# Placing turned query tiles with four transfers instead of six, and turning them one unit earlier, in both attentions of a two-layer trunk

## The chip, the cores and the metric

One Trainium2 chip, one core. The metric is device time in microseconds (us) of one execution; smaller is better. The kernel before was timed three times: 3293.59, 3291.07 and 3286.45 us, median 3291.07.

## The reference, cut to what matters

The program is one step of a two-layer trunk on 1024 latent tokens and 128 context tokens. The change touches only the attention of each layer. Cut to that, the reference computes:

```python
def blocked_gqa(q, k, v):                      # layer 0: 8 query heads, 2 key/value heads, head width 64
    def one_block(qblk):                       # 128 queries at a time
        s = jnp.einsum('bqkgd,bskd->bkgqs', qblk, k) * D ** -0.5
        pr = jax.nn.softmax(s, axis=-1)
        return jnp.einsum('bkgqs,bskd->bqkgd', pr, v)

def blocked_diff_attention(q, k, v, lam):      # layer 1: 8 heads, two maps each, value width 128
    def one_block(qblk):
        s = jnp.einsum('bqphd,bsphd->bphqs', qblk, k) * D ** -0.5
        pr = jax.nn.softmax(s, axis=-1)
        w = pr[:, 0] - lam * pr[:, 1]
        return jnp.einsum('bhqs,bshe->bqhe', w, v)
```

Latent queries see 256 cached keys and 1024 latent keys (1280); context queries see the 128 context keys. Everything is float32.

## The kernel before, in words

**Split products.** A float32 factor is kept as two parts, high and low. For the scores (L1311 to L1331) the keys of a head lie in `ks` as 128 rows: 64 rows of high parts and below them 64 rows of low parts. The queries lie in `qst` for two slots `v`, and two matmuls, one per slot, add up in one PSUM tile. Before the change slot 0 holds high over low and slot 1 low over high, so that the two matmuls together form all four products of a high or low query part with a high or low key part.

**Groups, tiles, units.** `attention` (L906) is built twice. Layer 0 (`l == 0`) has two groups of four query heads that share one key head; layer 1 has four groups of two heads with two maps each. Inside a group the tokens are projected tile by tile (nine tiles of 128 tokens: eight latent, one context); then the scores, the softmax and the products with the values go by units. A unit is one head of one query tile: four units per tile in layer 0, two units of two maps in layer 1. `program` (L1037) is the order of a group and is replayed by each engine with its own functions; `unit_0` (L990) and `unit_1` (L1012) are the order inside a unit. In unit `u` TensorE (PE) makes the scores of unit `u + 1`, turns (transposes against an identity) the probabilities of unit `u - 2` (layer 0) or `u - 1` (layer 1), and makes the product with the values; in layer 0 that product and the exponentials are made in even units only, for two units at once. ACT copies the turned probabilities out of PSUM (`attn_pt`, L1429) and makes the exponentials (L1496), DVE takes the maxima (L1703), scales the probabilities (L1715) or mixes the two maps (L1721), and reads out the product (L1729, L1731). Turned things share two PSUM banks in alternation (`next_bank`, L1240): whoever takes a bank waits until what lay in it two uses ago was read.

**The way of a query tile.** `stage` on PE (L1304) transposes the queries of tile `qt` (L1308); `stage` on ACT (L1478) copies them to `q_turned` (L1483); `split_queries` on POOL (L1168) makes the high and the low part in `q_parts` (L1172, L1174), after the transfers of the tile before have landed; `place_queries` on SP (L1110) sends the parts to `qst[qt % 2]`; the first scores of the tile wait for these transfers (L1316). There are six transfers: two of 128 KB (L1117, L1118) and four of 64 KB (L1120, L1121, one per slot). Tiles 0 and 1 are staged while tokens are still projected (`STAGED_AT`). `stage_after` (L1065) says after which unit the later ones are: in layer 0 tile `t + 1` in unit `4t + 1`, in layer 1 tile `t + 2` in unit `2t + 1`.

**The queue of SP.** `group` on SP (L1123 to L1156) goes in order: loads of cached keys and values; placements of tiles 0 and 1; a wait until the weights of this group are used (L1139); the weight loads of the next group (`pre.load`, 1.5 MB in layer 0 and 3 MB in layer 1) or, in the last group, three pieces of the output weights (`out_ahead`); the stores of the new keys and values; placements of tiles 2 to 8.

```python
    def stage_after(u):
        qt = u // per_tile + (1, 2)[l]
        return qt if u % per_tile == 1 and qt >= 2 and qt < NT else None
```

## Time and profile before

| what | value |
|---|---|
| median of 3 runs | 3291.07 us (3286.45 to 3293.59) |
| the profiled execution | 3292.2 us |
| its span | 3290.4 us |
| mean granted TensorE clock | 0.984 |
| the two groups of attention 0 | about 262 to 600 us of the span |
| the four groups of attention 1 | about 1630 to 2360 us of the span |

The span runs from the first to the last instruction; the execution's own time is 1.8 us longer. Of an engine the profile gives busy time and, in the view of waits, for whom it stood idle. "PEld" is TensorE's weight load, which runs beside its matmuls ("PE"), whose ends are modelled; a wait in front of a matmul therefore shows twice, once in each, with slightly different lengths.

### The profile page before, as it was taken

How to read it: one execution, taken by the hardware profiler on the slowest of the kernel's cores; microseconds unless marked ns; L12 is line 12 of the kernel's file. 1: busy time of each engine (PE TensorE's matmuls, PEld its weight loads, DVE VectorE, ACT ScalarE, POOL GpSimd, SP SyncE). 2: the span in 40 equal slices, each digit the busy share in tenths (PEclk: the TensorE clock that was granted, in tenths of full speed). 3: DMA queues.
4: the chain of work that ended last, by engine and by line, in shares of the span. 5: the costliest groups of instructions: out<-in, count | busy, mean ns of one | idle time of the engine just before them, and what ended most of it. 6: DMA issues, size and time to landing. Idle time of an engine off the chain costs nothing. (4 is left out here: it accounts for less than half of the span.)

```text
span 3290.4 us, 55637 instructions
## 1 busy us (share of the span) xinstructions
PE 3086.6 (94%) x19944; PEld 2384.8 (72%) x19944; DVE 2218.8 (67%) x2691; ACT 1847.0 (56%) x2625; POOL 696.1 (21%) x587
## 2 busy tenths in 40 slices
PE   5998989998999999997999999999997999999999
PEld 4767777774767777675887888888885677767776
DVE  4777676557666666665777776867747766666666
ACT  3555747434666665563466483755733666566564
POOL 1101010001233223321322122222200222332221
PEclk9999999998999999999999999999998999999999
DMA  7231111439888888887021210302245888888885
GB/s 235 87 131 47 33 39 33 146 139 380 297 285 305 289 303 285 293 296 237 15 75 27 67 35 13 87 14 55 72 166 213 300 294 300 287 287 309 292 295 155
DMA packets 240092, 593.71 MB, mean 180 GB/s; under 512 B 38883, under 2 KB 90280, under 8 KB 239656
## 3 DMA queue, kind: packets, MB, share of 16 engines
q1 hardware_dynamic: 229534, 557.54, 48.2%
q0 software_dynamic: 9472, 33.57, 4.3%
q8 instruction: 109, 1.79, 0.2%
q14 instruction: 71, 0.58, 0.1%
q10 hardware_dynamic: 906, 0.23, 0.0%
HBM read 524.00 MB, written 38.94 MB: 171 GB/s over the span
## 5 line engine op out<-in xcount | busy, mean ns | idle before, releaser
L2193 DVE TENSOR_TENSOR moe_lo<-moe_raw,moeg_hi 128x2048 fp32r<-128x2048 f32 x384 | 882.2, 2325 | 289.5 <-ACT moeg_hi L2190 153.8
L2190 ACT CAST moeg_hi<-moe_raw 128x2048 fp32r<-128x2048 f32 x384 | 729.6, 1913 | 437.5 <-PE psum L2596 320.8
L1208 PE MATMUL psum<-attn_w_hi,attn_hs 128*128 128x512 f32 (+2 forms) x1424 | 370.2, 343 | 16.3 <-DVE attn_hs L1587 11.3
L1703 DVE TENSOR_REDUCE attn_neg_max<-psum 128x1 f32<-128x1280 f32 (+1 forms) x216 | 292.1, 1354 | 117.0 <-PE psum L1328 115.6
L1328 PE MATMUL psum<-attn_ks,attn_qst 128*128 128x512 f32 (+2 forms) x1200 | 305.5, 376 | 48.8 <-DMA attn_qst<-attn_q_parts 25.3
L1496 ACT ACTIVATE attn_e<-psum,attn_neg_max 128x1280 f32<-128x1280 f32 (+1 forms) x216 | 265.1, 1228 | 94.8 <-DVE attn_neg_max L1703 91.3
L1208 PEld LDWEIGHTS psum<-attn_w_hi,attn_hs 128*128 128x128 f32 x1424 | 250.8, 190 | 48.4 <-DVE attn_hs L1587 12.2
L1328 PEld LDWEIGHTS psum<-attn_ks,attn_qst 128*128 128x128 f32 x1200 | 203.1, 190 | 87.6 <-DMA attn_qst<-attn_q_parts 26.2
L2596 PE MATMUL psum<-moe_lo,moeh_x_hi 128*128 128x512 f32 x960 | 262.0, 395 | 0.0
L2596 PE MATMUL psum<-moeg_hi,moeh_x_hi 128*128 128x512 f32 x960 | 261.5, 394 | 0.0
L2596 PE MATMUL psum<-moeg_hi,moeh_x_lo 128*128 128x512 f32 x960 | 260.5, 393 | 0.0
L1208 PE MATMUL psum<-attn_w_lo,attn_hs 128*128 128x256 f32 (+2 forms) x712 | 241.4, 339 | 0.0
L2181 PE MATMUL psum<-moe_raw,moeh_xc 128*32 128x512 f32 x2048 | 234.3, 598 | 0.0
L1429 ACT COPY attn_pt<-psum 128x512 f32<-128x512 f32 (+2 forms) x400 | 190.8, 506 | 64.0 <-PE psum L1341 57.6
L2596 PEld LDWEIGHTS psum<-moeg_hi,moeh_x_hi 128*128 128x128 f32 x960 | 177.7, 188 | 51.2 <-issue 14.0
L2596 PEld LDWEIGHTS psum<-moeg_hi,moeh_x_lo 128*128 128x128 f32 x960 | 180.1, 188 | 42.3
L2596 PEld LDWEIGHTS psum<-moe_lo,moeh_x_hi 128*128 128x128 f32 x960 | 180.4, 188 | 41.1
L1341 PE MATMUL psum<-ident,attn_e 128*128 128x128 f32 x1296 | 196.3, 279 | 12.0 <-ACT attn_pt L1429 7.7
L1341 PEld LDWEIGHTS psum<-ident,attn_e 128*128 128x128 f32 x1296 | 145.5, 141 | 41.2 <-issue 20.7
L2174 POOL COPY moeh_xc<-moe_x_ctx 128x64 f32 (+1 forms) x64 | 126.5, 2007 | 217.6 <-PE psum L2181 191.5
L2486 POOL CAST moeh_x_hi<-moeh_x_tmp 128x1024 fp32r<-128x1024 f32 x30 | 32.0, 1065 | 639.9 <-ACT moeh_x_tmp L2681 639.9
L1188 POOL TENSOR_TENSOR rstd<-ssq,neg_half 128x8 f32<-128x8 f32 (+1 forms) x54 | 80.1, 1484 | 406.2 <-DVE ssq L1619 406.2
(359 smaller groups left out, 5433.1 us busy)
## 6 DMA issues: line engine op xcount, KB each, us to landing
moe_raw<-in_l_w_gate SPq DMA_DIRECT2D x256, 512.0 KB, 4.1
moe_raw<-in_l_w_up SPq DMA_DIRECT2D x256, 512.0 KB, 5.2
moe_raw<-in_l_w_down SPq DMA_DIRECT2D x128, 1024.0 KB, 6.2
ada_w<-in_l_ada_w SPq DMA_DIRECT2D x19, 1024.0 KB, 13.7
attn_qst<-attn_q_parts SPq DMA_DIRECT2D x108, 128.0 KB, 2.4
attn_qst<-attn_q_parts SPq DMA_DIRECT2D x216, 64.0 KB, 2.1
ada1h_w<-in_l_ada_w SPq DMA_DIRECT2D x9, 1024.0 KB, 10.9
lru_ada<-in_l_ada_w SPq DMA_DIRECT2D x8, 1024.0 KB, 7.7
```

The source lines that it names most:

```text
L1188: pool.tensor_tensor(m.rstd[:, 0:nz], m.ssq[:, 0:nz], m.neg_half[:, 0:nz], ALU.pow).then_inc(s["rstd"], 1)
L1208: last = pe.matmul(out, hs[t % 2][:, part, k, :], right, start=(i == 0 and n == 0), stop=(i == KB - 1 and n == 2))
L1328: last = pe.matmul(m.psum[:, into:into + step], query_map(u // per_tile, qm, v), ks[:, km, col:col + step], start=(v == 0), stop=(v == 1))
L1341: last = pe.transpose(m.psum[:, at + (i - b) * P:at + (i - b + 1) * P], src[:, i * P:(i + 1) * P], m.ident[:, :])
L1429: act.copy(out, src).then_inc(s["turn_read"], 1)
L1496: act.activation(out[:, 0:hi - lo], m.psum[:, score_at(n):score_at(n) + hi - lo], ACT.Exp, bias=neg_max[:, n:n + 1], accum_out=sums[:, n:n ...
L1703: dve.tensor_reduce(neg_max[:, n:n + 1], m.psum[:, score_at(n):score_at(n) + hi - lo], AX.X, ALU.max, negate=True).then_inc(s["maxed"], 1)
L2174: last = pool.tensor_copy(dst[:, :, j, :], mm.x_ctx[:, :, ds(e * 8 + j * P, 8)])
L2181: last = pe.matmul(m.psum[32 * g:32 * g + 32, 6 * BANK:7 * BANK], mm.xc[:, k, :], mm.raw[k][:, g // 2, (g % 2) * BANK:(g % 2 + 1) * BANK], ...
L2190: act.copy(mm.hi[slot % 4][:, :, :], mm.raw[slot][:, :, :]).then_inc(mm.s["hi_ready"], 1)
L2193: dve.tensor_tensor(mm.lo[slot][:, :, :], mm.raw[slot][:, :, :], mm.hi[slot % 4][:, :, :].bitcast(F32), ALU.subtract).then_inc(mm.s["lo_re ...
L2596: last = pe.matmul(m.psum[:, at:at + BANK], x[:, k, :], w[:, j, half * BANK:(half + 1) * BANK], start=(k == 0 and i == 0), stop=(k == KB - ...
```

## The change

It does four things in both attentions. The slots of `qst` now hold the high part twice (in both halves of the rows) and the low part twice, so a tile is placed by four transfers of 128 KB, and the counter per tile goes from 96 to 64. A tile is turned one unit sooner: in layer 0 tile `t + 1` in unit `4t`, in layer 1 tile `t + 2` in unit `2t`. Before placing tiles from 2 on, SP waits until all scores that read the buffer (those of tile `qt - 2`) are made. And on SP the stores and the placement of tile 2 come ahead of the weight loads of the next group.

```diff
@@ -980 +980 @@
-    PLACED = 6 * 16
+    PLACED = 4 * 16
@@ -1065 +1065 @@
-        return qt if u % per_tile == 1 and qt >= 2 and qt < NT else None
+        return qt if u % per_tile == 0 and qt >= 2 and qt < NT else None
@@ -1112 +1112 @@ place_queries
                 wait_value(m, sp, s["q_split"], j * NT + (qt + 1))
                 if qt == 1:
                     wait_value(m, sp, s["ssq"], j * NT + NT)
+                if qt >= 2:
+                    wait_value(m, sp, s["scored"], j * nmaps + (qt - 1) * per_tile * maps)
                 top, low = slice(0, HD), slice(HD, P)
                 to, parts = qst[qt % 2][:, :, :, :, :].bitcast(F32), q_parts[:, :, :, :].bitcast(F32)
-                sp.dma_start(to[top, 0, :, :, :], parts[top, :, :, :]).then_inc(s["q_placed"], 16)
-                sp.dma_start(to[low, 1, :, :, :], parts[low, :, :, :]).then_inc(s["q_placed"], 16)
-                for v in range(2):
-                    sp.dma_start(to[low, 0, v, :, :], parts[top, 1 - v, :, :]).then_inc(s["q_placed"], 16)
-                    sp.dma_start(to[top, 1, v, :, :], parts[low, 1 - v, :, :]).then_inc(s["q_placed"], 16)
+                for i, of in enumerate((top, low)):
+                    for half in (top, low):
+                        sp.dma_start(to[half, i, :, :, :], parts[of, :, :, :]).then_inc(s["q_placed"], 16)
@@ -1136 +1136 @@ group on SP
                 for qt in range(2):
                     place_queries(j, qt)
-                wait_value(m, sp, s["w_used"], j + 1)
-                if last:
-                    out_ahead(sp)
-                else:
-                    pre.load(sp, j + 1)
-
                 wait_value(m, sp, s["k_new"], j + 1)
                 wait_value(m, sp, s["v_copied"], j * NT + NT)
...
-                for qt in range(2, NT):
+                place_queries(j, 2)
+                wait_value(m, sp, s["w_used"], j + 1)
+                if last:
+                    out_ahead(sp)
+                else:
+                    pre.load(sp, j + 1)
+                for qt in range(3, NT):
                     place_queries(j, qt)
```

## Rows read from the trace of the kernel before

**Rows 1.** The page: busy time of the engines, and the group of the score matmuls.

```profile
PE 3086.6 (94%) x19944; PEld 2384.8 (72%) x19944; DVE 2218.8 (67%) x2691; ACT 1847.0 (56%) x2625; POOL 696.1 (21%) x587
...
L1328 PE MATMUL psum<-attn_ks,attn_qst 128*128 128x512 f32 (+2 forms) x1200 | 305.5, 376 | 48.8 <-DMA attn_qst<-attn_q_parts 25.3
```

**Rows 2.** Waits of PE and PEld in both groups of attention 0: total us, times, longest.

```profile
PE psum L1328 <- DMA attn_qst<-attn_q_parts: 21.8, 14, 2.8
...
PEld psum L1328 <- DMA attn_qst<-attn_q_parts: 25.1, 14, 3.0
```

**Rows 3.** Timeline, one tile boundary of attention 0: start us, duration us, [idle before].

```profile
334.68 0.37 ACT L1483 COPY attn_q_turned<-psum 128x256 f32<-128x256 f32 x1 [0.36 <-PE psum L1308]
...
336.75 0.46 SPq L1117 DMA_DIRECT2D attn_qst<-attn_q_parts  x1
...
339.82 0.60 SPq L1121 DMA_DIRECT2D attn_qst<-attn_q_parts  x1
...
341.93 0.30 PEld L1328 LDWEIGHTS psum<-attn_ks,attn_qst 128*128 128x128 f32 x2 [1.50 <-DMA attn_qst<-attn_q_parts]
341.93 0.73 PE L1328 MATMUL psum<-attn_ks,attn_qst 128*128 128x512 f32 x2 [1.26 <-DMA attn_qst<-attn_q_parts]
```

**Rows 4.** Timeline, the even unit after it, without a turned query tile.

```profile
345.56 1.34 ACT L1496 ACTIVATE attn_e<-psum,attn_neg_max 128x1280 f32<-128x1280 f32 x1
345.88 2.40 PE L1358 MATMUL psum<-attn_pt,attn_v 128*64 128x128 f32 x40
345.99 1.49 DVE L1703 TENSOR_REDUCE attn_neg_max<-psum 128x1 f32<-128x1280 f32 x1 [0.88 <-PE psum L1328]
...
347.63 0.89 DVE L1715 TENSOR_SCALAR attn_e<-attn_e,attn_inv 128x1280 f32<-128x1280 f32 x1
348.21 0.97 PEld L1341 LDWEIGHTS psum<-ident,attn_e 128*128 128x128 f32 x8 [0.17 <-issue]
...
348.43 0.28 DVE L1729 COPY region<-psum 128x128 f32<-128x128 f32 x1
```

**Rows 5.** Busy time in one tile of attention 0, two of attention 1: PE, PEld, DVE, ACT, POOL.

```profile
341.93:358.10 16.17, 14.95 (x146) 12.49 (x146) 10.38 (x14) 11.74 (x21) 1.14 (x2) 1.00 0.14 33
1695.42:1708.30 12.88, 12.32 (x91) 11.00 (x90) 10.95 (x14) 10.54 (x24) 3.49 (x7) 1.00 0.18 42
1683.77:1695.42 11.65, 11.65 (x88) 10.84 (x88) 9.68 (x13) 9.78 (x21) 3.55 (x6) 1.00 0.20 47
```

**Rows 6.** The page's DMA issues: KB each, median us from issue to landing.

```profile
attn_qst<-attn_q_parts SPq DMA_DIRECT2D x108, 128.0 KB, 2.4
attn_qst<-attn_q_parts SPq DMA_DIRECT2D x216, 64.0 KB, 2.1
```

**Rows 7.** Waits of PE in the four groups of attention 1.

```profile
PE psum L1328 <- DMA attn_qst<-attn_q_parts: 3.6, 8, 0.8
```

**Rows 8.** Timeline, one tile boundary of attention 1.

```profile
1901.77 1.40 PE L1328 MATMUL psum<-attn_ks,attn_qst 128*128 128x512 f32 x6
...
1911.94 0.46 SPq L1117 DMA_DIRECT2D attn_qst<-attn_q_parts  x1
...
1915.01 0.60 SPq L1121 DMA_DIRECT2D attn_qst<-attn_q_parts  x1
...
1918.32 1.22 PEld L1328 LDWEIGHTS psum<-attn_ks,attn_qst 128*128 128x128 f32 x6 [0.66 <-issue]
1918.33 1.42 PE L1328 MATMUL psum<-attn_ks,attn_qst 128*128 128x512 f32 x6 [0.47 <-DMA attn_qst<-attn_q_parts]
```

**Rows 9.** Timeline, the first units of a group of attention 1, SP and PE.

```profile
1668.61 5.58 SPq L866 DMA_DIRECT2D attnw_w<-in_l_w_in  x5
...
1671.13 1.42 PE L1328 MATMUL psum<-attn_ks,attn_qst 128*128 128x512 f32 x6 [2.40 <-ACT attn_e L1496]
```

**Rows 10.** Windows there, last columns: clock, DMA share, GB/s moved.

```profile
1680.00:1682.00 2.00, 2.00 (x16) 1.87 (x15) 1.85 (x4) 1.99 (x5) 0.00 (x0) 1.00 1.11 336
1682.00:1684.00 2.00, 1.74 (x15) 1.56 (x14) 2.00 (x3) 0.25 (x1) 0.00 (x0) 1.00 0.42 86
```

## The prediction, made before the changed kernel was run

> **What bounds the kernel now.** I read the page first. PE is busy 94% of the span, and the score matmuls are the only large PE group with a transfer named as what they waited for: 48.8 us idle before them, 25.3 of it until `attn_qst` had landed [rows 1]. That is what the change can win on PE, so the next view was the waits, cut by attention. In attention 0 the wait stands 14 times, once for each of tiles 2 to 8 in both groups: 21.8 us in front of the matmuls, 25.1 in front of their weight loads [rows 2]. In attention 1 it stands 8 times, 3.6 us in all [rows 7]. Then the timeline at one boundary of attention 0: the turned tile is copied at 334.68, POOL splits it, SP issues six transfers from 336.75 to 340.42, and the scores start at 341.93, after PE had idled 1.26 us and PEld 1.50 [rows 3]. Last the windows: in the tile from 341.93 PE is busy 14.95 of 16.17 us, DVE 10.38, ACT 11.74 [rows 5]. So here PE sets the pace, its one hole is this wait, and the engines that would be next have 3 us or more to spare per tile. In attention 1 PE is busy 12.32 of 12.88 us in a tile that opens a wait, and all of 11.65 us in one without [rows 5].
>
> **Two transfers fewer.** Issues on SP follow each other every 0.64 us (four steps and a last issue of 0.60 lead from 336.75 to 340.42; the first is shorter) [rows 3], so two fewer end 2 x 0.64 = 1.28 us sooner. The last is now one of 128 KB, 2.4 us to landing against 2.1 [rows 6]: 0.3 back. Alone this would cut each wait of attention 0 by about 1.0 of 1.26 to 1.50 us. Bytes are the same, 512 KB per tile.
>
> **One unit sooner, attention 0.** A tile is four units in 16.17 us [rows 5], so a unit is about 4 us, and the placement lands 4 us sooner beside the 1.0 us above. The longest wait of the 14 is 2.8 to 3.0 us [rows 2]. All 14 go, with 2 us or more to spare. Their worth lies between 21.8 (PE) and 25.1 us (PEld) [rows 2], since matmul ends are modelled; I take the middle, **23.4 us**. The turning itself (two matmuls on PE, a copy of 0.37 us on ACT, the two operations on POOL) stays as often as it was.
>
> **What the move costs.** In attention 0 the turned tile moves from an odd unit into an even one, and the even one makes the exponentials of two units and the product with the values. ACT works in order: the copy, 0.37 us plus 0.36 of waiting for PE [rows 3], now stands ahead of the exponentials. Costing: in an even unit without it the exponential starts at 345.56 and takes 1.34, the maximum beside it ends at 347.48, the scaling runs from 347.63 and the copy of the values' product from 348.43, for which PE's next unit waits in part (0.97 us for eight weight loads) [rows 4]. PE comes 0.34 us later with everything because it turns the queries first; that is no loss, the odd unit gets it back. The maximum then ends at 347.8; the exponential, 0.73 later, ends at 347.6, and the reading of its sum and the reciprocal follow, so I estimate the scaling to start near 348.2 in place of the 348.0 that PE's shift alone gives, some 0.25 us late, and the copy that PE waits for with it. So 14 x 0.25 = **3.5 us back**. Bounds: nothing, if the bank has slack, and the full 0.36 + 0.37 = 0.73 us, 14 x 0.73 = 10.2 us, if the copy holds the pair from end to end. I take 0.25 since DVE's maximum [rows 4] hides most of it.
>
> On this the Trainium skill speaks against the change: TensorE: Matmul & The Clock Gate, "Architectural detail: the array is 16× 32×32, not 1× 128×128", says that ACT and DVE are strict FIFO, so what stands behind a waiting copy waits with it. The row agrees as far as the copy's own 0.36 us; by the rule alone the sum would be 6.7 us worse than mine.
>
> **One unit sooner, attention 1.** All units have one form, so the turning costs the same in either. The placement moves from 1911.94 [rows 8] by half a tile, 5.8 to 6.4 us [rows 5], to about 1905.8. The added wait on SP is for the last scores that read the buffer; these start at 1901.77 and end at 1903.2 [rows 8], moved at most by the two turning matmuls, so it is met 2 us before POOL has the parts. Behind it on SP stands only this placement. The placement then lands 7 us or more before the scores that now start at 1918.32 after 0.47 (PE) or 0.66 us (PEld) [rows 8]. All 8 waits go. Lower bound 3.6 us [rows 7]; upper bound by pitch, a tile with a wait against one without: 8 x (12.88 - 11.65) = 9.8 us [rows 5], though that second tile also has less to do (ACT 9.78 against 10.54). I take **4 us**, near the row that names the wait.
>
> **Order on SP.** Tile 2 is turned in unit 0 in attention 1, where PE has a hole of 2.40 us right behind [rows 9], so nothing is lost. The stores and tile 2's placement now come first: the copy of tile 2 follows the exponential that PE waits for until 1671.13, the first issue comes 2.07 us after a copy starts (334.68 to 336.75) [rows 3], four issues take 2.5, so the weight loads begin near 1675.8 in place of 1668.61 [rows 9], 7 us later. Their stream kept the DMA engines full until about 1682.5 [rows 9, 10], 14 us after its start; it now ends near 1690. Tile 3 is placed behind it, but its scores start at 1695.42 [rows 5], so 5 us are spare. The weights are wanted from unit 15 on, at about 6 us a unit. In attention 0 half as many bytes move. I cost this at zero; if the cover failed, a few us in three groups. The stores go sooner, which nobody waits for.
>
> **Sum.** 23.4 - 3.5 + 4 = 23.9 us. The profiled execution took 3292.2 us (span 3290.4), so 3268.3. That execution is 1.1 us above the median shown, 3291.07; against the median the forecast is **3267 us**. Nothing after either attention starts by a clock of its own, so the gain is not given back later.
>
> **The rivals.**
>
> *The copy holds the pair (0.13).* The 0.73 us passes through whole, 14 times, and the waits are worth their lower figure: 21.8 - 10.2 + 3.6 = 15.2 us, 3276 us; with nothing from attention 1, 3280. For it: ACT's order, above. Against it: ACT has 4.4 us idle per tile [rows 5].
>
> *Attention 1 gives more (0.07).* Its tiles with a wait fall to 11.65 us and the moved copy is free: 25.1 + 9.8 = 34.9 us, 3256. Against it: PE has no holes beyond the named ones.
>
> *No change (0.04).* The waits go, and another limit of the same pace appears, or the added wait on SP and POOL's wait for the tile before keep the placement where it was: about 3291. Against it: DVE's and ACT's busy time [rows 5], and the end of the scores at 1903.2 [rows 8].
>
> *Slower (0.04).* The place is the even unit of attention 0: if ACT's copy makes both exponentials miss their slot, PE stands at the next bank for as long as the values' product runs, 2.40 us [rows 4], 14 times: 33.6 us against 23.4 + 3.6 won, net 6.6 us, 3298 us. It decides from 27.0 / 14 = 1.9 us per turned tile. Against it: the copy is 0.37 us, and the same copy in the odd unit delays nobody by more than 0.36.
>
> **How the numbers follow.** The forecast has 0.72; its own range, from 25.1 + 9.8 us without cost to 21.8 - 3.5 us with nothing from attention 1, is 3256 to 3273. The first rival stretches it to 3280. The range is **3256 to 3281**; no change, slower and the edges of the others are left out, under 2 in 10. A measurement of this kernel tells about 0.2%, 6.6 us, from no change. Faster by more than that has the forecast, the first two rivals and little else: 0.92; within it 0.04; slower 0.04.
>
> **What would show it.** Right: the wait of the score matmuls for `attn_qst` is gone from both attentions or below 1 us in all; 216 issues of 128 KB and none of 64 KB; a tile of attention 0 takes 14.8 to 15.2 us in place of 16.17, with PE busy throughout; in even units that turn a tile the copy stands between the `attn_pt` copies and the exponential, and PE's next weight loads wait a little longer for L1729; attention 1's groups shorten by about 1 us each. Wrong: a tile of attention 0 above 15.6 us, PE idle for L1729 or L1496 in each tile, or a wait for `attn_qst` that stays at tile 3 in attention 1, behind the weights.

## The result, and the profile after

The changed kernel takes 3260.25 us in the median of four runs (3258.65 to 3264.07), the kernel before, run beside it, 3292.33 us (3286.45 to 3294.76): a ratio of 0.9907, 95% interval 0.989 to 0.9924, or about 31 us less (25 to 36). The profiled execution took 3264.07 us (span 3262.1) against 3292.2 (span 3290.4), 28.1 us less. The forecast of 3267 lies 7 us above the median, inside its range and in the right direction; it had 24 us as the gain. The profiled execution of the changed kernel is the slowest of its four, so the traces hold 28 of the 31 us.

From the page after, the busy times, the group of the score matmuls and the placements, to be held against [rows 1] and [rows 6]:

```profile
PE 3085.7 (95%) x19944; PEld 2384.4 (73%) x19944; DVE 2220.4 (68%) x2691; ACT 1845.8 (57%) x2625; POOL 693.6 (21%) x587
...
L1328 PE MATMUL psum<-attn_ks,attn_qst 128*128 128x512 f32 (+2 forms) x1200 | 306.6, 377 | 23.5 <-ACT attn_e L1496 21.4
...
attn_qst<-attn_q_parts SPq DMA_DIRECT2D x216, 128.0 KB, 2.4
```

PE does the same work; the idle time before the score matmuls fell from 48.8 to 23.5 us, and no transfer is named in it any more. 25.3 us of waiting for `attn_qst` became nothing.

The waits of PE in attention 0, after (engine, line, waited for: us, times, longest), against [rows 2]:

```profile
PE psum L1341 <- ACT attn_pt L1429: 5.6, 5, 3.1
PE psum L1208 <- DVE attn_hs L1587: 5.6, 7, 1.0
PE psum L1328 <- ACT attn_e L1496: 4.0, 3, 1.9
```

The 21.8 us for `attn_qst` are not there, and no other wait of the matmuls grew by more than 0.3 us (`L1341` on `attn_pt` had 6.3 us before, `L1208` 5.6, `L1328` on `attn_e` 3.7). In front of the weight loads one wait grew, from 1.0 us in 3 times to 3.3 us in 12, for DVE's reading of the product; a row of it stands below.

The timeline after, around one turn in attention 0 (start us, duration us, [idle before]), against [rows 3] and [rows 4]. It is the even unit now:

```profile
323.77 0.37 PEld L1308 LDWEIGHTS psum<-ident,attn_qtok 128*128 128x128 f32 x2
...
324.47 0.37 ACT L1483 COPY attn_q_turned<-psum 128x256 f32<-128x256 f32 x1 [0.37 <-PE psum L1308]
324.65 1.49 DVE L1703 TENSOR_REDUCE attn_neg_max<-psum 128x1 f32<-128x1280 f32 x1 [1.10 <-PE psum L1328]
324.74 1.34 ACT L1496 ACTIVATE attn_e<-psum,attn_neg_max 128x1280 f32<-128x1280 f32 x1
...
326.43 0.89 DVE L1715 TENSOR_SCALAR attn_e<-attn_e,attn_inv 128x1280 f32<-128x1280 f32 x1
326.59 2.39 SPq L1121 DMA_DIRECT2D attn_qst<-attn_q_parts  x4
326.87 0.42 PEld L1341 LDWEIGHTS psum<-ident,attn_e 128*128 128x128 f32 x4 [0.17 <-issue]
327.24 0.28 DVE L1729 COPY region<-psum 128x128 f32<-128x128 f32 x1
327.57 0.42 PEld L1341 LDWEIGHTS psum<-ident,attn_e 128*128 128x128 f32 x4 [0.28 <-DVE region L1729]
...
335.20 0.30 PEld L1328 LDWEIGHTS psum<-attn_ks,attn_qst 128*128 128x128 f32 x2
```

The four placements are issued by 328.98, and the first scores of the new tile start at 335.20 without a wait (last row). The price of the move is in the row at 327.57: 0.28 us in which PE's weight loads wait until DVE has read the values' product. The copy is ahead of the exponential on ACT, so the exponential's sum, the scaling and that reading come later. The windows show tiles that follow one another, two of attention 0 and two of attention 1 (busy PE, PEld, DVE, ACT, POOL, then clock, DMA share, GB/s), against [rows 5]:

```profile
323.77:338.61 14.84, 14.80 (x148) 12.48 (x147) 10.48 (x14) 11.76 (x22) 1.13 (x2) 1.00 0.16 36
338.61:353.45 14.84, 14.80 (x148) 12.48 (x147) 10.47 (x14) 11.75 (x22) 1.13 (x2) 1.00 0.16 38
1874.18:1886.30 12.12, 12.08 (x88) 10.95 (x89) 10.19 (x14) 10.41 (x24) 3.32 (x6) 1.00 0.19 45
1886.30:1898.42 12.12, 12.09 (x88) 10.94 (x88) 10.18 (x14) 10.50 (x24) 3.32 (x6) 1.00 0.19 45
```

A tile of attention 0 takes 14.84 us where it took 16.17, with PE busy in 14.80 of them.

**Where the time went.** Each profiled execution can be cut at rows of SP: the first placement of attention 0, the loads of `out_w` that follow each attention, the first placement of attention 1, and the first load of cached keys in groups 2 to 4 of attention 1. In us:

| kernel | attention 0 | between | attention 1 | its groups |
|---|---|---|---|---|
| before | 350.2 | 1020.6 | 736.8 | 144.7, 197.1, 197.7, 197.3 |
| after | 327.6 | 1016.5 | 734.6 | 143.3, 197.5, 197.1, 196.8 |

What lies ahead of attention 0 and behind attention 1 changed by 1.0 us down and 1.6 us up. The spans differ by 28.3 us: 22.6 are attention 0, 2.2 attention 1, and 4.0 come from a stretch that the change does not touch; the same cuts in the experiments tell whether those 4.0 us go with the change.

A group of attention 1 can be cut once more, at the start of DVE's first and last maximum (L1703). Between these two lie its units, and from the last maximum of a group to the first of the next lie the end of its units and the projections of the next group. The units of the four groups took 415.5 us before and 412.1 after, 3.4 less. The three stretches between groups took 275.9 us before and 277.1 after, 1.2 more, and all of that is in the first of them (92.6 and 93.8 us). There PE's hole ahead of the second tile of projections is 2.23 us long where it was 1.57, and the granted clock fell behind it; before, it fell at another place of the stretch (1775 us). The run with the old order on SP has more on this hole.

### The profile page after: what moved, and what is told of

Same layout as the page of the kernel before. It is cut to its first block and busy times, and to the rows that moved or that the text cites. A ratio compares the mean times of both kernels' runs of the same rounds, so it can differ in the third digit from the quotient of the medians.

```text
span 3262.1 us, 55592 instructions
## 1 busy us (share of the span) xinstructions
PE 3085.7 (95%) x19944; PEld 2384.4 (73%) x19944; DVE 2220.4 (68%) x2691; ACT 1845.8 (57%) x2625; POOL 693.6 (21%) x587
## 5 line engine op out<-in xcount | busy, mean ns | idle before, releaser
L1208 PE MATMUL psum<-attn_w_hi,attn_hs 128*128 128x512 f32 (+2 forms) x1424 | 370.8, 343 | 16.9 <-DVE attn_hs L1587 11.0
L1703 DVE TENSOR_REDUCE attn_neg_max<-psum 128x1 f32<-128x1280 f32 (+1 forms) x216 | 292.2, 1355 | 86.3 <-PE psum L1328 84.8
L1328 PE MATMUL psum<-attn_ks,attn_qst 128*128 128x512 f32 (+2 forms) x1200 | 306.6, 377 | 23.5 <-ACT attn_e L1496 21.4
L1208 PEld LDWEIGHTS psum<-attn_w_hi,attn_hs 128*128 128x128 f32 x1424 | 250.5, 190 | 49.7 <-DVE attn_hs L1587 12.1
L1328 PEld LDWEIGHTS psum<-attn_ks,attn_qst 128*128 128x128 f32 x1200 | 204.1, 191 | 59.5 <-ACT attn_e L1496 26.7
L1208 PE MATMUL psum<-attn_w_lo,attn_hs 128*128 128x256 f32 (+2 forms) x712 | 241.1, 339 | 0.0
L1341 PE MATMUL psum<-ident,attn_e 128*128 128x128 f32 x1296 | 198.9, 281 | 11.4 <-ACT attn_pt L1429 7.0
L1341 PEld LDWEIGHTS psum<-ident,attn_e 128*128 128x128 f32 x1296 | 147.6, 143 | 41.4 <-issue 22.9
```

Of the source, the lines that this page charges most:

```text
L1208: last = pe.matmul(out, hs[t % 2][:, part, k, :], right, start=(i == 0 and n == 0), stop=(i == KB - 1 and n == 2))
L1328: last = pe.matmul(m.psum[:, into:into + step], query_map(u // per_tile, qm, v), ks[:, km, col:col + step], start=(v == 0), stop=(v == 1))
L1341: last = pe.transpose(m.psum[:, at + (i - b) * P:at + (i - b + 1) * P], src[:, i * P:(i + 1) * P], m.ident[:, :])
L1703: dve.tensor_reduce(neg_max[:, n:n + 1], m.psum[:, score_at(n):score_at(n) + hi - lo], AX.X, ALU.max, negate=True).then_inc(s["maxed"], 1)
```

## The experiments

The theory after the result: the whole gain is the waits of attention 0, and turning one unit sooner is what removes them; the four transfers and the order on SP are then worth nothing for themselves. Rivals: the fewer transfers carry it; the order on SP has a share; the move's cost is another than the rows say.

### One part of the change at a time

In the first four kernels a part that is "off" is as before. The diffs of this document are cut, and set against the changed kernel where nothing else is said. Four transfers alone:

```diff
-        return qt if u % per_tile == 0 and qt >= 2 and qt < NT else None
+        return qt if u % per_tile == 1 and qt >= 2 and qt < NT else None
...
-                place_queries(j, 2)
                 wait_value(m, sp, s["w_used"], j + 1)
...
-                for qt in range(3, NT):
+                for qt in range(2, NT):
```

(The weight loads stand ahead of the stores again, and SP's wait for the scores of tile `qt - 2` is gone too.) Expected: 

> Only the layout and the number of transfers change: four of 128 KB, turned in the same unit as before, same order on SP. My theory (a placement is simply late by 1.26 to 1.5 us in attention 0, and the transfers start late because the tile is turned late): the last issue comes 1.28 us sooner and lands 0.3 slower, so each of the 14 waits falls by about 1.0 us, to 0.3 to 0.5, the first of group 0 from 2.8 to 1.8. The sum of PE's waits for attn_qst in attention 0 falls from 21.8 to about 8 us, the kernel gains 13 to 16 us. Rival (the landing time is set by the DMA engines' work on 512 KB, not by the issues): waits stay above 1.0 us each, and the gain is below 5 us.

Measured: 3278.52 us (3271.53 to 3280.4) beside 3294.31, ratio 0.9951 [0.9934, 0.9968]: 16 us less. Its waits in attention 0, PE and PEld (L1343 is L1328 there):

```profile
PE psum L1343 <- DMA attn_qst<-attn_q_parts: 7.0, 13, 1.5
```
```profile
PEld psum L1343 <- DMA attn_qst<-attn_q_parts: 11.0, 14, 1.7
```

Against 21.8 and 25.1 us [rows 2] each of the 14 waits is 1.0 us shorter, as two issues fewer give. Attention 0 takes 338.4 us, 11.8 less than before. In attention 1, where the longest of the 8 waits was 0.8 us [rows 7], four transfers alone remove all of them: its units take 412.9 us against 415.5 before.

Turned sooner alone, with six transfers and, not shown in the diff, the weight loads ahead of the stores as before:

```diff
-    PLACED = 4 * 16
+    PLACED = 6 * 16
...
-                for i, of in enumerate((top, low)):
-                    for half in (top, low):
-                        sp.dma_start(to[half, i, :, :, :], parts[of, :, :, :]).then_inc(s["q_placed"], 16)
+                sp.dma_start(to[top, 0, :, :, :], parts[top, :, :, :]).then_inc(s["q_placed"], 16)
...
```

Expected: 

> Only the unit changes (and the wait for the scores that keeps it safe): six transfers, old order on SP. My theory: the placement comes 4 us sooner in attention 0 and 6 us sooner in attention 1, more than any wait, so all waits for attn_qst go and the gain is that of the whole change, 28 to 32 us; the four transfers add nothing on top, except possibly at the third tile of attention 1, which is behind the weight loads. Rival (both parts are needed, or six issues on SP hold up something else): waits stay, and the gain is under 22 us.

Measured: 3261.62 us (3260.38 to 3264.82), ratio 0.9907 [0.9889, 0.9926]: all of the gain, with six transfers of a tile. Attention 0 takes 327.6 us, the same as the whole change.

The order on SP alone, turned in the odd unit and with six transfers as before (this diff is against the kernel before):

```diff
-                wait_value(m, sp, s["w_used"], j + 1)
...
+                place_queries(j, 2)
+                wait_value(m, sp, s["w_used"], j + 1)
...
-                for qt in range(2, NT):
+                for qt in range(3, NT):
```

Expected: 

> Only the order on SP changes: stores and the placement of the third tile ahead of the weight loads, six transfers, old unit. My theory: the third tile's wait in group 0 of attention 0 falls from 2.8 to about 1.3 us if the stores and weights in front of it were what made it longer; in attention 1 the third tile's 0.3 to 0.8 us goes; all in all 1 to 3 us, no more than a measurement can tell from nothing. Rival (the weight loads now fall on the placements of later tiles): new waits of over 1 us at the fourth tile, and the kernel is slower by 3 us or more.

Measured: 3301.71 us (3291.6 to 3318.21, ten runs), ratio 1.0027 [1.001, 1.0044]: 9 us slower (3 to 14), where 1 to 3 us less was expected; the rival came true. The timeline of SP and the scores behind it:

```profile
1675.72 0.51 SPq L1125 DMA_DIRECT2D attn_qst<-attn_q_parts  x1
...
1679.72 5.67 SPq L866 DMA_DIRECT2D attnw_w<-in_l_w_in  x5
1687.26 1.23 SPq L1125 DMA_DIRECT2D attn_qst<-attn_q_parts  x1
...
1691.10 0.77 SPq L1129 DMA_DIRECT2D attn_qst<-attn_q_parts  x1
```
```profile
1696.26 2.50 PE L1343 MATMUL psum<-attn_ks,attn_qst 128*128 128x512 f32 x6 [3.26 <-DMA attn_qst<-attn_q_parts]
```

The next tile's parts are issued from 1687.26, right behind 3 MB of weights, and the last of them is there only some 4.4 us after its issue ended at 1691.87. PE waits 3.26 us and then gets a lower clock, which costs more (the section on the hardware). Groups 1 to 3 of attention 1 take 148.2, 201.0 and 198.5 us, against 144.7, 197.1 and 197.7 before. This part by itself is a loss; turned one unit sooner, the same tile is placed before it is wanted and nothing waits: in the whole change's first group its last transfer lands at 1662.92 and its scores start at 1667.9.

The change in attention 0 alone (`l == 1` as before in all three parts). Expected: 

> The whole change in attention 0, nothing of it in attention 1. By the milestones of the two traces attention 0 gives 22.6 us and attention 1 2.2 us. My theory: the gain is 22 to 24 us over the kernel before, and the rest of the 28 to 32 us measured is attention 1's 2 us and scatter from run to run outside the attentions. Rival (attention 1 or something behind it gives more than its own milestones show): the gain is under 20 us, or the gap to the whole change is over 6 us.

Measured: 3266.08 us (3262.89 to 3269.16), ratio 0.9914 [0.9896, 0.9933]: 28 us less; it was expected at 22 to 24, and this difference is not explained. Its trace has 329.6 us for attention 0 (20.6 less than before; one fall of the clock more than the whole change has there), 735.6 for attention 1, with 415.5 in the units as before, and 2.9 less between the attentions.

### The order on SP, taken out of the whole change

The edit is the second half of the first diff above. Expected: 

> The whole change but for the order on SP: the weight loads go ahead of the stores and of the third tile's placement, as before. My theory after the first runs: once tiles are turned a unit sooner, the order is worth nothing either way, because neither the third nor the fourth tile is near its deadline: within 3 us of the whole change (3257 to 3264 us), no waits for attn_qst. Rival (the new order costs attention 1 the 1 to 1.5 us per group by which the middle groups were shorter in the runs with the old order): 4 us faster than the whole change, with middle groups of attention 1 at 195.5 to 196.2 us in place of 197.3.

Measured: 3260.21 us (3257.49 to 3263.18), ratio 0.9896 [0.9874, 0.9917], no difference from the whole change. In its trace groups 2 and 3 of attention 1 take 195.1 us each against 197.5 and 197.1. That looked like a cost of 2 us a group in what the new order changes, but there it isn't: the units take the same 412.1 us, and the difference lies in the projections, ahead of the group's stores. The windows there (last columns: clock, DMA share, GB/s), first with the old order, then the whole change:

```profile
1754.00:1757.00 3.00, 2.27 (x20) 2.03 (x18) 1.84 (x3) 0.93 (x2) 0.00 (x0) 1.00 0.03 8
1757.00:1760.00 3.00, 2.34 (x10) 1.94 (x11) 0.73 (x3) 0.84 (x2) 0.00 (x0) 1.00 0.04 11
1760.00:1763.00 3.00, 3.00 (x15) 2.41 (x14) 1.83 (x6) 2.26 (x4) 0.79 (x1) 1.00 0.00 0
```
```profile
1754.00:1757.00 3.00, 1.30 (x12) 1.07 (x10) 2.55 (x5) 0.95 (x2) 0.00 (x0) 1.00 0.04 11
1757.00:1760.00 3.00, 2.46 (x6) 1.99 (x7) 0.00 (x0) 1.80 (x3) 0.00 (x0) 0.57 0.03 8
1760.00:1763.00 3.00, 3.00 (x13) 2.40 (x12) 2.72 (x7) 1.29 (x3) 1.65 (x1) 0.87 0.00 0
```

The clock fell in one and not in the other. Ahead of it PE stands at the start of the group's second tile of projections, with no releaser named, longer in the whole change than with the old order (first the whole change, then the old order):

```profile
1757.54 0.79 PE L1208 MATMUL psum<-attn_w_hi,attn_hs 128*128 128x512 f32 x1 [2.23 <-issue]
```
```profile
1757.66 0.49 PE L1223 MATMUL psum<-attn_w_hi,attn_hs 128*128 128x512 f32 x1 [1.39 <-issue]
```

The same place stands in groups 2 and 3 of all fourteen traces. Its idle time lies between 1.33 and 2.23 us; in ten of the 28 groups the granted clock was 0.57 to 0.66 in the 4 us behind, and these are the ten in which PE had stood longest. From the last maximum of the group in front to the first of this one, these ten took 93.4 to 93.8 us, and the eleven without any fall of the clock 91.5 to 91.9. Is it the order on SP? Four kernels with the new order have the fall in both groups (the whole change, the odd unit, the copy three times, POOL's order), and the two that turn sooner with the old order (this one, and sooner alone) have it in neither. Against that, four kernels with the new order have it in neither group (order alone, turn late, both that turn early), turn at the end has it in one, and group 3 of the kernel before has it with the old order. So the order alone does not decide it, but a share of it, up to 4 us in the two groups, is not excluded; the totals show none. What makes this idle time long or short is open.

### What the move costs

The turn of attention 0 in the odd unit in front, half a tile further ahead than before the change:

```diff
-        qt = u // per_tile + (1, 2)[l]
-        return qt if u % per_tile == 0 and qt >= 2 and qt < NT else None
+        qt = (u + 1) // per_tile + 1 if l == 0 else u // per_tile + 2
+        return qt if (u + 1 if l == 0 else u) % per_tile == 0 and qt >= 2 and qt < NT else None
```

Expected: 

> In attention 0 tile t + 1 is turned in unit 4t - 1, an odd unit, one more unit sooner than in the changed kernel; all else as there. My theory: turning in the even unit lengthens the pair by 0.36 us (the exponentials and the copy of the product come late), in an odd unit by 0.22, as the pitches of the two traces say, so a tile of attention 0 goes from 14.84 to 14.70 us and the kernel gains 2 us, at the edge of what can be told; the trace shows it. Rival (what a turned tile costs is only PE's own 0.34 us wherever it stands): the tile stays at 14.84.

Measured: 3259.19 us (3256.03 to 3265.05), ratio 0.9891 [0.9869, 0.9912]. The turns in its trace:

```profile
322.34 0.38 PE L1323 MATMUL psum<-ident,attn_qtok 128*128 128x128 f32 x2
337.03 0.38 PE L1323 MATMUL psum<-ident,attn_qtok 128*128 128x128 f32 x2
351.73 0.38 PE L1323 MATMUL psum<-ident,attn_qtok 128*128 128x128 f32 x2
```

A tile of 14.70 us in place of 14.84: the even unit costs 0.14 us a tile, which would be 2 us in 14, and that is too little for the total to show. Attention 0 as a whole takes 326.6 us here, 1.0 less than in the whole change, and in the two later kernels with the same edit 327.9 and 328.0, so only the length of a tile shows this gain.

The other way, ACT's copy three times over where attention 0 stages a tile from 2 on:

```diff
+                    for _ in range(2 if l == 0 and qt >= 2 else 0):
+                        act.copy(out, turned)
+                        act.drain()
                     act.copy(out, turned).then_inc(s["q_copied"], 1)
```

Expected: 

> The changed kernel, but in attention 0 ACT copies each turned tile from 2 on three times over (the same copy, each with a drain), so its queue is held some 0.8 us longer in 14 even units. My theory: in the changed kernel the first exponential's sum is read at the moment DVE's maximum beside it ends, so the slack is used up and more delay goes through DVE's scaling and its copy of the product to PE one to one: a tile takes 14.84 + 0.7 to 0.9 us, the kernel loses 9 to 13 us. Rival (ACT has slack here, the copy's place costs nothing): under 3 us lost.

Measured: 3274.46 us (3272.72 to 3278.52), ratio 0.9939 [0.9918, 0.9959]: 14 us more than the whole change. The wait of PE's weight loads for DVE's reading (L1729, there L1747):

```profile
331.98 0.42 PEld L1356 LDWEIGHTS psum<-ident,attn_e 128*128 128x128 f32 x4 [1.15 <-DVE region L1747]
```

1.15 us against 0.28 above, 0.87 more a tile and 12 us in 14, and a tile of 15.70 us. The exponential starts 1.61 us after PE's turn (327.53 to 329.14), in the whole change 0.74 (324.00 to 324.74), also 0.87 more: what ACT is given beyond the first copy comes through one to one. Of the first copy's 0.73 us only 0.14 shows, and the maximum, which ran beside it, is what can have covered the rest.

### Where the turn can stand in attention 1

In attention 1 PE's weight loads wait at the turn for ACT to free the bank, after the change (7.6 us in 18 times) as before it (9.7 us in 21). From the changed kernel:

```profile
1874.18 0.20 PEld L1308 LDWEIGHTS psum<-ident,attn_qtok 128*128 128x128 f32 x2 [0.47 <-ACT attn_pt L1429]
```

Four kernels move the turn within `unit_1`, to three places. Behind the second map's scores and so, on ACT, behind the exponential:

```diff
-        if stage_after(u) is not None:
-            make["stage"](stage_after(u))
         if u >= 1:
             make["exps"](u + 1, 0)
         if u + 1 < units:
             make["scores"](u + 1, 1, 1)
             make["scores"](u + 1, 1, 2)
+        if stage_after(u) is not None:
+            make["stage"](stage_after(u))
```

Expected: 

> In attention 1 the query tile is turned, copied and split behind the last scores of the unit in place of behind the first piece of the second map's scores; the unit is the same as in the changed kernel. My theory: attention 1 gained only 2 us of the 4 forecast because the unit that turns a tile is held at its PSUM bank (PE's weight load for it stands 0.47 us for ACT's copy of the turned probabilities), so it takes 6.36 us where the other takes 5.75; with 0.8 us of score matmuls in front that wait goes, a tile of attention 1 falls from 12.12 to 11.7 to 11.9 us, and the kernel gains 5 to 10 us. Rival (ACT's own queue sets the 12.12 us, PE's wait is only where it shows): the wait goes and the tile stays within 0.1 us of 12.12.

Measured: 3290.74 us (3288.54 to 3292.45, ten runs), ratio 0.999 [0.998, 0.9999], nearly the whole gain lost: a miss. The product with the values (L1385 there) takes the same two banks:

```profile
1884.53 2.47 PE L1385 MATMUL psum<-attn_v,attn_pt 128*128 128x128 f32 x20 [1.48 <-ACT attn_q_turned L1498]
```

It waits 1.48 us until ACT, behind the exponential, has copied the turned tile. A tile takes 13.57 us (1870.96 to 1884.53), and attention 1 761.2.

Ahead of the probabilities:

```diff
+        if stage_after(u) is not None:
+            make["stage"](stage_after(u))
         if lag <= u < units + lag:
             make["turn_probs"](u - lag, 0)
         if u + 1 < units:
             make["scores"](u + 1, 1, 0)
-        if stage_after(u) is not None:
-            make["stage"](stage_after(u))
```

Expected: 

> The whole change, and in attention 1 the turn of the next tile's queries put ahead of the unit's probabilities (TensorE, and with it the ScalarE copy out of the bank), where it now stands behind them. Theory: in the changed kernel TensorE's weight loads wait 0.4 to 0.5 us at that place for ScalarE to free the bank (2.5 us in a group, six times), and the even unit takes 6.36 us against 5.75 without a turned tile; an earlier bank has been read long before, so this wait goes: 24 times 0.3 to 0.47 us, 7 to 11 us less than the whole change (3249 to 3254 us), and a tile of attention 1 takes 11.6 to 11.8 us instead of 12.12. Rival 1: ScalarE, not the bank, sets the pitch of the unit; its copy of 0.37 us is merely moved ahead of the copies of the probabilities, and the tile stays at 12.1 us, the run within 2 us of the whole change. Rival 2: the copy delays the probabilities and with them the values, as behind the exponential: a tile over 12.4 us, and slower than the whole change by 7 us or more.

Measured: 3275.27 us (3266.05 to 3277.09), ratio 0.9929 [0.9914, 0.9945]: a miss again, rival 2 came true. The wait for the bank at the turn is gone, and a longer one stands where the second half of the probabilities wants the turn's bank:

```profile
1881.86 0.42 PEld L1356 LDWEIGHTS psum<-ident,attn_e 128*128 128x128 f32 x4 [0.86 <-ACT attn_q_turned L1498]
```

0.86 us in place of 0.47; a tile of 12.57 us (1881.86 to 1894.43, where the same row comes again) against 12.12, times 24 tiles 10.8 us. The units of attention 1 are 9.6 us longer than after and attention 1 as a whole 7.5. The medians stand 15 us apart; 4.4 us of the profiled execution are between the attentions, and the rest is not explained. The same with attention 0's turn in the odd unit. Expected: 

> The edit of the run before, together with the turn of attention 0 moved into the unit in front (the odd one). Theory: the two gains stand in different attentions and add: the 7 to 11 us of the early turn in attention 1, and the 1 to 2 us that the odd unit gave in attention 0 (tile 14.70 us instead of 14.84), so 3247 to 3252 us. Rival: neither reaches the total; within 2 us of the whole change.

Measured: 3272.83 us (3271.96 to 3276.3), ratio 0.9936 [0.9922, 0.9949]: a miss with the edit that it contains (units of attention 1 421.4 us).

GpSimd's order, for itself:

```diff
-                    if stage_after(u) is not None:
-                        split_queries(j, stage_after(u))
                     if l == 1 and u >= OUT_LAG:
                         normal_of_out(j, u - OUT_LAG)
+                    if stage_after(u) is not None:
+                        split_queries(j, stage_after(u))
```

Expected: 

> The whole change, with GpSimd's normalisation of an output ahead of its split of the next tile's queries in attention 1. In the changed kernel ScalarE waits for GpSimd at the output's normalisation for 14.9 us in all (12.5 before), a few times a group. Theory: these waits are covered, since ScalarE has 16 us of other waits in a group and TensorE waits for none of it: within 3 us of the whole change. Rival: they lie on the path, because ScalarE's queue frees TensorE's banks: up to 10 us less.

Measured: 3263.86 us (3263.41 to 3264.03), ratio 0.9906 [0.9891, 0.9921]; attention 1 734.1 us against 734.6, its units 411.9 against 412.1. The median is 3.6 us above that of the whole change, where 3 was expected, with ratios that can't be told apart; the units show that ACT's waits for POOL are covered.

From the two misses I took a rule: a place is free only if the bank it takes was read, if whoever takes the bank next comes after ACT's copy, and if ACT has idle time there. In the trace after, the end of the odd unit, behind the values, is such a place (ACT idles 0.87 us ahead of an exponential once a tile). The last kernel turns there, with attention 0 in the odd unit and POOL's order as above:

```diff
-        if stage_after(u) is not None:
+        if u == 0:
             make["stage"](stage_after(u))
...
-        make["exps"](u + 1, 1)
         if values_after(u) is not None:
             make["values"](values_after(u))
+        if u and stage_after(u) is not None:
+            make["stage"](stage_after(u))
+        make["exps"](u + 1, 1)
...
-        qt = u // per_tile + (1, 2)[l]
-        return qt if u % per_tile == 0 and qt >= 2 and qt < NT else None
+        qt = (u + 1) // per_tile + (1, 2)[l]
+        first = l == 1 and u == 0
+        return 2 if first else qt if (u + 1) % per_tile == 0 and qt >= 2 and qt < NT else None
```

Expected: 

> The whole change with three more edits: attention 0 turns in the odd unit in front; in attention 1 tiles 3 and on are turned at the very end of the odd unit in front, behind its values and ahead of its second exponential; GpSimd's normalisation of an output stands ahead of the split. Theory, read from the changed kernel: at that place the bank that the turn takes was read 0.2 us before, ScalarE sits idle 0.87 us ahead of the exponential that follows (it waits for the maximum) and can hold its copy of 0.37 us there, and the values' bank, which the next probabilities then take sooner, is read 0.5 us before they want it. So no engine waits for the turn: a tile of attention 1 takes 11.5 to 11.7 us instead of 12.12, times 20 turned tiles 8 to 12 us, and 1 to 2 us from the odd unit: 3247 to 3252 us. Rival 1: the banks come in another order, and TensorE's probabilities wait for ScalarE's copy or VectorE's reading of the output, 0.5 us or more a tile, as in the run before last: 3260 to 3275 us. Rival 2: the transfers come no later and nothing waits, but the pitch is ScalarE's: within 2 us of the whole change.

Measured: 3257.07 us (3254.6 to 3263.86), where 3247 to 3252 was expected, ratio 0.9895 [0.9879, 0.9911], the lowest median of all kernels, though its interval overlaps that of the whole change (0.989 to 0.9924), so that 3 us between them are not shown by the totals. The tile shows a gain:

```profile
1868.70 0.38 PE L1326 MATMUL psum<-ident,attn_qtok 128*128 128x128 f32 x2
...
1880.55 0.38 PE L1326 MATMUL psum<-ident,attn_qtok 128*128 128x128 f32 x2
```
```profile
1881.03 0.37 ACT L1501 COPY attn_q_turned<-psum 128x256 f32<-128x256 f32 x1 [0.62 <-PE psum L1326]
1881.29 1.34 ACT L1514 ACTIVATE attn_e<-psum,attn_neg_max 128x1280 f32<-128x1280 f32 x1
```

A tile takes 11.85 us in place of 12.12, and from tile 4 on no wait of PE for a bank at the turn is left. At tile 3's turn, once in each group, a new one stands, 0.55 to 0.70 us and 2.6 in all, since the bank held turned keys that ACT had yet to copy:

```profile
1648.49 0.44 PE L1326 MATMUL psum<-ident,attn_qtok 128*128 128x128 f32 x2 [0.67 <-ACT attn_ks L1447]
```

The units of attention 1 take 408.1 us, 4.0 less than after, where 20 x 0.27 would be 5.4; attention 1 as a whole takes 729.5, 5.1 less, the other 1.1 from projections in which the clock fell at other places. That is half of what was expected or less: the expectation took the turned tile down to a tile without one, but PE's own work for the turn stays (0.23 us of weight loads and 0.38 us of matmuls, the latter in part beside the scores), and so does the wait at tile 3.

### The same cuts through all traces

| kernel | attention 0 | between | attention 1 |
|---|---|---|---|
| before | 350.2 | 1020.6 | 736.8 |
| four transfers alone | 338.4 | 1019.8 | 732.3 |
| sooner alone | 327.6 | 1016.4 | 732.0 |
| order on SP alone | 351.7 | 1016.6 | 745.0 |
| attention 0 alone | 329.6 | 1017.7 | 735.6 |
| whole change | 327.6 | 1016.5 | 734.6 |
| whole, old order | 327.5 | 1016.3 | 731.1 |
| odd unit | 326.6 | 1017.3 | 734.2 |
| copy three times | 341.2 | 1016.2 | 735.5 |
| turn late | 327.6 | 1016.0 | 761.2 |
| turn early | 327.5 | 1020.9 | 742.1 |
| turn early, odd unit | 327.9 | 1016.6 | 740.9 |
| POOL's order | 327.4 | 1016.4 | 734.1 |
| turn at the end | 328.0 | 1016.6 | 729.5 |

The stretch between the attentions takes 1016.0 to 1017.7 us in eleven of these executions and 1019.8 to 1020.9 in three: with nothing changed in attention 0 (before), with a part of it (four transfers), and with all of it (turn early), while the order alone, whose attention 0 is as before, has 1016.6. So the 4.0 us between do not go with the change. In the kernel before, the clock lost there (one less the granted clock, summed over the stretch) is 27.3 us of full clock against 23.9 after; in turn early it is 23.9 and the stretch long all the same. So the clock can be a cause of the one and not of the other, and what sets the length is open.

## Why the prediction was right, point by point

**The 14 waits of attention 0.** Right that all go, and that turning sooner is what does it. Taking the middle between PE and PEld was the step that was off: at the boundary shown the tile fell by 16.17 - 14.84 = 1.33 us and the move cost 0.14, so the wait was worth 1.47 us, PEld's 1.50 and not PE's 1.26 [rows 3]. Over the attention, 22.6 us gained and 14 x 0.14 = 2.0 paid (if every tile pays it) make 24.6 us, near PEld's 25.1 and not the 23.4 taken [rows 2].

**Two transfers fewer.** Right: 1.0 us a wait. Alone they gave 16 us in the total, 11.8 of it in attention 0. Once the turn comes sooner they are worth nothing.

**What the move costs.** Right in kind, size off: 0.14 us a tile, 2.0 us if all 14 pay it, where 0.25 and 3.5 were taken. More of the copy is hidden than was estimated. The Trainium skill's rule that ACT's and DVE's queues are strict FIFO (TensorE: Matmul & The Clock Gate, "Architectural detail: the array is 16× 32×32, not 1× 128×128") is seen at full price where nothing hides it: with the copy three times over PE waited 0.87 us longer a tile. By the rule alone the change would have cost the 0.73 us a tile of the prediction's rows; it cost 0.14.

**Attention 1.** All 8 waits went, but the stretch is only 2.2 us shorter, where 4 was taken. The upper bound of 9.8 us was badly drawn: it set a tile of 12.88 against one of 11.65, and those have different contents. The turns of the kernel before are the better measure:

```profile
1896.27 0.44 PE L1308 MATMUL psum<-ident,attn_qtok 128*128 128x128 f32 x2
1908.39 0.44 PE L1308 MATMUL psum<-ident,attn_qtok 128*128 128x128 f32 x2
1920.93 0.38 PE L1308 MATMUL psum<-ident,attn_qtok 128*128 128x128 f32 x2
```

A tile took 12.12 us there without the wait, exactly as after, and 12.54 with it: 0.42 a time, 3.4 us in 8. The units are 3.4 us shorter, so the waits are worth what the lower bound said, 3.6, and the 4 taken was near. The 1.2 us by which the whole stretch falls short stand in the projections of group 2, with their longer hole and the fall of the clock behind it, which the prediction didn't look for. With the same waits gone attention 1 took 731.1 to 735.5 us in five traces (whole change, old order, odd unit, POOL's order, copy three times), its units 411.9 to 412.4.

**Order on SP.** Costed at nothing, and right for the sum, with the reason given: tile 3 had 5 us to spare (1662.92 to 1667.9). What covered it was the sooner turn, and the text did not say so: without it the order costs 9 us, at the place that the prediction named as the one to look at. That it also has a share in the clock's falls in the projections is not excluded.

**What was not forecast.** Of the 28.3 us between the two spans, 4.0 are a shorter stretch between the attentions. The sum was 23.9; attention 0 gave 22.6 where 19.9 stood, attention 1 2.2 where 4 stood, and these 4.0 us, less 0.6 at the two ends, make the rest. So 23.9 against 24.8 in the two attentions is closer than the single terms were: 2.7 us too little in one and 1.8 too much in the other. And that the median fell by 31 us, 6 more than the attentions gave, is not explained; the forecast is low by that, and it was inside the range all the same. The rivals fell: the copy does not hold the pair (0.14 of 0.73), no new limit appeared, and nothing missed its slot.

## What to carry to other kernels

Where a short transfer is waited for at every tile, start its chain sooner before making it cheaper: in attention 0 the sooner start took all 14 waits, fewer transfers only 1 us of each. (Where the waits are under 1 us, as in attention 1, either is enough.) Before moving a step that goes through a shared bank, write down who had the bank, who wants it next, and what stands ahead of the copy that frees it on its engine; the same 0.37 us copy cost 0.14 us a tile in attention 0's even unit against the odd one, and in attention 1, against the place of the whole change, 0.45 or 1.45 more and 0.27 less, depending on where it stood. And an edit that is free beside another one may be a loss alone (the order on SP), so parts are to be costed in the company they will have.

## What the runs showed of the hardware

**A wait costs more than its length.** In the kernel with the order alone, around the wait of 3.26 us (clock in the third column from the end):

```profile
1692.00:1695.00 3.00, 1.00 (x9) 0.81 (x8) 1.64 (x2) 2.21 (x5) 0.71 (x2) 1.00 0.53 103
1695.00:1698.00 3.00, 1.74 (x4) 1.46 (x5) 0.00 (x0) 0.12 (x1) 0.00 (x0) 0.70 0.01 5
1698.00:1701.00 3.00, 3.00 (x17) 2.71 (x17) 2.06 (x4) 1.20 (x3) 0.00 (x0) 0.73 0.00 0
```

PE stood still, and the granted clock went from 2.4 GHz to 1.2 GHz for part of two windows of 3 us: 0.30 x 3 + 0.27 x 3 = 1.7 us of full clock. The six score matmuls behind the wait took 2.50 us instead of 1.40. In the whole change, in the projections of group 2, 0.57 and 0.87 make the same: 0.43 x 3 + 0.13 x 3 = 1.7 us. What such a fall costs in time depends on its place. In the projections the stretch is 2 us longer with it, the longer hole included (93.4 to 93.8 against 91.5 to 91.9). At the start of the units, where PE waits for ACT in any case [rows 9], it cost nothing: the first group's units took 103.84 us in the whole change, with a fall from 1644 on, and 103.80 with the old order on SP, without one.

**A fall can stand behind a short hole.** The same instructions ran in part at 1.2 GHz in one trace and at 2.4 in another, after PE had idled 2.23 and 1.39 us (rows at 1757 above). Other idle time stands near: in the 3 us ahead PE was busy 1.30 and 2.27 us, so it is not shown that the one hole decides. Such falls, and 4 us between the attentions, are a large part of what single traces of this kernel differ by, so 2 us in one stretch of one trace should be looked up in the clock before they are put down to an edit.

**A placement right behind 3 MB of loads** landed 5.0 us after its last issue (1691.10 to 1696.13; the scores start at 1696.26), where the median from issue to landing on the page before is 2.1 to 2.4 us [rows 6]. In the first group of the whole change it was 5.5 us (1657.47 to 1662.92), and nothing waited.
